# One transfer of 1 MB in place of two of 512 KB for the weight sums of each block unit

## The reference

```
def sq_relu_mlp(xn, w_in, w_out):
    h = jax.nn.relu(xn @ w_in)          # 1024 -> 4096
    return (h * h) @ w_out              # 4096 -> 1024

for i in range(2):
    h = h + attention_i(rms_norm(h, norm_mix_g[i]))
    h = h + sq_relu_mlp(rms_norm(h, norm_mlp_g[i]), mlp_w_in[i], mlp_w_out[i])
return rms_norm(h, norm_final_g)
```

## Time and profile before

| | before |
|---|---|
| median of 3 runs | 1864.57 us (1864.54 to 1865.13) |
| the profiled execution | 1863.85 us |
| its span, first to last instruction | 1862.1 us |
| PE busy | 1850.7 us, 99% of the span |
| DVE busy | 1311.2 us, 70% |
| ACT busy | 953.2 us, 51% |
| POOL busy | 222.8 us, 12% |
| granted clock of TensorE, mean | 0.999 |
| weight sums loaded by SP | 68 transfers of 512 KB, median 5.4 us from issue to landing |

### The profile page before, as it was taken

One profiled execution on the slowest core, in us unless ns is written; L12 is line 12 of the kernel. 1 busy time (PEld: TensorE's weight loads), 2 busy tenths in 40 slices (PEclk: granted clock), 3 DMA queues, 4 the chain that ended last, 5 costly groups with the idle time before them and its releaser, 6 DMA issues.

```text
span 1862.1 us, 28582 instructions
## 1 busy us (share of the span) xinstructions
PE 1850.7 (99%) x10747; PEld 1548.4 (83%) x10747; DVE 1311.2 (70%) x1816; ACT 953.2 (51%) x1222; POOL 222.8 (12%) x254
## 2 busy tenths in 40 slices
PE   9999999999999999999999999999999999999998
PEld 7788878888888887877888999988778788999997
DVE  7767775677357757556575788887788658588878
ACT  6392464545234343544443555555667754456464
POOL 0011122212211123111200000002101220000000
PEclk9999999999999999999999999999999999999999
DMA  6226213897888538786454353538335642435441
GB/s 243 90 83 194 68 65 94 208 216 176 201 204 204 125 110 200 164 192 159 138 134 158 112 194 119 187 114 221 110 102 153 141 132 96 153 119 187 144 179 69
DMA packets 128085, 277.43 MB, mean 149 GB/s; under 512 B 7389, under 2 KB 78941, under 8 KB 121696
## 3 DMA queue, kind: packets, MB, share of 16 engines
q1 hardware_dynamic: 95744, 187.19, 29.5%
q0 software_dynamic: 31936, 88.41, 22.7%
q10 hardware_dynamic: 288, 0.26, 0.0%
HBM read 271.53 MB, written 73.51 MB: 185 GB/s over the span
## 4 chain that ended last, share of the span: by engine, by line
PE 95%; DVE 2%; ACT 1%; DMA 1%; issue 0%; ACTq 0%; DVEq 0%
PE bank L1191 21%; PE bank L1189 21%; PE bank L1190 21%; PE bank L1629 6%; PE bank L1630 6%; PE bank L1631 6%; PE bank L1317 2%; PE bank L1934 2%; PE bank L1916 1%; DMA raw<-in_a_w_qkv 1%; PE bank L1323 1%; PE bank L1805 1%; PE bank L1806 1%; PE bank L1807 1%; PE bank L1793 1%; PE bank L1740 1%
## 5 line engine op out<-in xcount | busy, mean ns | idle before, releaser
L1189 PE MATMUL bank<-n_hi,w_hi 128*128 128x512 f32 x1054 | 425.0, 403 | 1.3 <-DVE w_lo L2030 1.3
L1191 PE MATMUL bank<-n_hi,w_lo 128*128 128x512 f32 x1054 | 417.9, 396 | 0.0
L1190 PE MATMUL bank<-n_lo,w_hi 128*128 128x512 f32 x1054 | 416.9, 396 | 0.0
L2024 ACT ACTIVATE w_hi<-raw 128x2048 fp32r<-128x2048 f32 (+2 forms) x111 | 207.4, 1868 | 343.0 <-PE bank L1191 327.5
L2030 DVE TENSOR_TENSOR w_lo<-raw,w_hi 128x2048 fp32r<-128x2048 f32 (+2 forms) x117 | 261.6, 2236 | 107.9 <-ACT w_hi L2024 106.0
L1190 PE MATMUL bank<-ff_lo,w_hi 128*128 128x512 f32 x688 | 271.6, 395 | 0.0
L1191 PE MATMUL bank<-ff_hi,w_lo 128*128 128x512 f32 x624 | 248.8, 399 | 0.0
L1189 PE MATMUL bank<-ff_hi,w_hi 128*128 128x512 f32 x624 | 245.2, 393 | 0.0
L1189 PEld LDWEIGHTS bank<-n_hi,w_hi 128*128 128x128 f32 x1054 | 198.0, 188 | 54.1 <-issue 5.0
L1190 PEld LDWEIGHTS bank<-n_lo,w_hi 128*128 128x128 f32 x1054 | 198.1, 188 | 48.8 <-issue 2.9
L1191 PEld LDWEIGHTS bank<-n_hi,w_lo 128*128 128x128 f32 x1054 | 197.9, 188 | 46.7
(11 more groups left out here) (467 smaller groups left out, 3319.1 us busy)
## 6 DMA issues: line engine op xcount, KB each, us to landing
weight_sums<-in_mlp_in POOLq DMA_DIRECT2D x72, 512.0 KB, 8.7
consts<-weight_sums SPq DMA_DIRECT2D x68, 512.0 KB, 5.4
raw<-in_w_up SPq DMA_DIRECT2D x22, 1024.0 KB, 7.3
raw<-in_mlp_out SPq DMA_DIRECT2D x22, 1024.0 KB, 4.8
raw<-in_mlp_in SPq DMA_DIRECT2D x24, 768.0 KB, 5.7
weight_sums<-weight_sums POOLq DMA_DIRECT2D x68, 256.0 KB, 5.9
weight_sums<-in_mlp_out POOLq DMA_DIRECT2D x30, 512.0 KB, 9.0
raw<-in_w_units SPq DMA_DIRECT2D x14, 1024.0 KB, 4.8
```

Source lines behind the costliest of these rows:

```text
L1189: nc.tensor.matmul(b[:, :], w_hi[:, j % 2, cols], hi, start=start, stop=False)
L1190: nc.tensor.matmul(b[:, :], w_hi[:, j % 2, cols], lo, start=False, stop=False)
L1191: return nc.tensor.matmul(b[:, :], w_lo[:, j % 2, cols], hi, start=False, stop=final)
L2024: act.activation(w_hi[:, s, cols], raw[:, s, cols], ACT.Copy).then_inc(hi_ready, 1)
```

## The change

Each block unit's sums come by one transfer of 1 MB, issued when both halves of the home are free, with one semaphore for each home in place of one for each home and half. ACT waits for the whole transfer ahead of either half.

```
-        sums_loaded, sums_made = {(i, op): sem("%s_loaded%d" % (op, i)) for i in range(2) for op in ("S23", "S14")}, sem("sums_made")
+        sums_loaded, sums_made = [sem("sums_loaded%d" % i) for i in range(2)], sem("sums_made")
...
         def summed(eng, m, op, u):
             i = sums_place(u)
-            eng.wait_ge(sums_loaded[i, op], 16 * sum(sums_place(v) == i and n <= SUM_ROW[m, u] for (_, v), n in SUM_ROW.items()))
+            eng.wait_ge(sums_loaded[i], 16 * sum(sums_place(v) == i and n <= SUM_ROW[m, u] for (_, v), n in SUM_ROW.items()))
...
                 for op in ("S23", "S14"):
                     sums_home_free(sp, m, op, u)
-                    to, cols = sum_piece(op, u), slice(0, 2 * SEQ) if op == "S23" else slice(2 * SEQ, 4 * SEQ)
-                    sp.dma_start(to, t["weight_sums"][SUM_ROW[m, u], :, cols]).then_inc(sums_loaded[sums_place(u), op], 16)
+                sp.dma_start(s_parts[sums_place(u)], t["weight_sums"][SUM_ROW[m, u]]).then_inc(sums_loaded[sums_place(u)], 16)
```

## The result

The changed kernel takes 1873.4 us in the median of six runs (1871.57 to 1874.29), the kernel before 1864.66 (1864.01 to 1865.4): a ratio of 1.0045, 95% interval 1.0034 to 1.0057, or 8.4 us (6.3 to 10.6). Losses in us are here the ratio times the kernel before; the two medians differ by 8.7. The forecast was 12.2 us slower, by a stall of TensorE at four places. The stalls are there, at those places, and are shorter than forecast. The profiled execution took 1874.29 us (span 1872.4), 10.4 us above the profiled one of before. One line went out of the code, so lines behind it are one lower (L2193 was L2194).

The account below looks back on a forecast made before the run. TensorE, busy 99% of the span, was taken to bound the kernel. Four border stalls of 2.5, 2.6, 4.2 and 2.9 us, together 12.2, on a median of 1864.6 gave 1876.8 us, range 1873 to 1881 (chance 0.62).

Parts of the forecast that it names:

- No idle time to win: Around the border of m = 1 and 2, TensorE is busy for all 34.00 us, so no gain can come there.
- SP's issue free: Removing 34 issues on SP, some 0.3 us each, 11 us in all, counts as nothing: SP is off the chain.
- 26 units covered: Units other than the four LATE and unit 0 after each: the longer transfer is covered and costs nothing.
- LATE: At four LATE units the transfer starts later; at the first border DVE moves 0.5 us, S1 in time by 0.4 us.
- Unit 0: Unit 0 of m = 2, 3, 6, 7: the late transfer delays S23, then A22 queued behind it; TensorE stalls 2.5 us at first.
- L1 + L2 - 7.8: TensorE's stall before A22 of unit 0 at each border: 2.5, 2.6, 4.2 and 2.9 us, together 12.2 us.
- L1: Time for 1 MB to land at the four LATE units: 4.9, 5.1, 5.6, 5.2 us.
- L2: Time for 1 MB to land at unit 0 after each LATE unit: 5.4, 5.3, 6.4, 5.5 us.
- the hidden rival: At the borders the longer transfer is hidden, perhaps helped by 8 KB rows: no change, 1864.6 us; chance 0.05.
- Half the stall: Rival: transfers take 4.7 us at each place, no cost of followers; 6.4 us slower, 1871.0 us; chance 0.13.
- Shared queue: Rival: at both transfers the second half adds 2.5 us, not 1.0; 12 us more, 1889 us; chance 0.08.
- The clock's fall: Rival: each of the four stalls brings the lower clock level; 9 us more, 1886 us; chance 0.10.

Follow-up runs that it names:

- the run with those units whole: Kernel before, with one 1 MB transfer for 26 units, two of 512 KB for the four LATE units and unit 0 after each: 1864.27 us, ratio 1.0002.
- the run with LATE alone: Kernel before, with one 1 MB transfer only for the four LATE units, the rest loaded as before: 1864.23 us, ratio 1.0002.
- the run of two transfers: Kernel before, two 512 KB transfers with a semaphore each, but both issued only when both halves are free: 1867.31 us, ratio 1.0017.
- the run with two rows of 4 KB: Changed kernel, the 1 MB described as two rows of 4 KB per partition; packets stayed as in the changed kernel: 1874.67 us, ratio 1.0054.
- The run with 5.4 us: Changed kernel, SP issuing unit 0's 1 MB after a LATE unit only when TensorE has ended LATE's last product: 1894.02 us, ratio 1.0159.

## Why the prediction was right, and where its size was off

*No idle time to win, SP's issue free, 26 units covered.* Right: the run with those units whole is at 1.0002.

*LATE.* Right in its mechanism: at the first border the low part of `S14` ended 6.62 us after LATE's first matmul in place of 6.17, so DVE moved by 0.45 us (forecast 0.5), S1 of LATE was in time, and the run with LATE alone loses nothing. The first matmul before and after, and the low part of `S14` after (1083.72 before):
```profile
1078.78 0.28 PE L1629 MATMUL bank<-ff_hi,w_hi 128*128 128x256 f32 x1
```
```profile
1078.49 0.28 PE L1628 MATMUL bank<-ff_hi,w_hi 128*128 128x256 f32 x1
```
```profile
1083.89 1.22 DVE L2193 TENSOR_TENSOR w_lo<-consts,w_hi 128x1024 fp32r<-128x1024 f32 x1
```

*Unit 0.* Right: place, releaser and order of the queues. The stall as L1 + L2 - 7.8 holds with the landings put in: at the first border 4.80 + 4.85 - 7.8 = 1.85, measured 1.94, and at the others it is as near, 0.1 us short. That nothing is late behind it holds as well. ACT's waits for sums are the 8 forecast: seven in the row below and the 7.36 us put down to TensorE, 43.3 us in all (forecast some 44).
```profile
ACT w_hi L2187 <- DMA consts<-weight_sums: 35.9, 7, 7.5
```
One sign failed: the granted clock did not stay at 1.00.

*The terms L1 and L2 are what was mis-sized.* I added 1.0 us for the second 512 KB to what a second half took in one execution, follower included: 4.9 to 5.6 and 5.3 to 6.4. They measured 4.7 to 4.9 and 4.8 to 5.1. So 1 MB beside followers lands nearly like the 1 MB of plain weights, and the 5.4 us of the third unit 0 were that execution's (4.1 to 4.7 us in three other runs with two halves there). The runs show a reason that I named under the hidden rival and put into no sum: the two halves went in packets of 4 KB, the whole goes in packets of 8 (SP's queue moves the same 187 MB in 90848 packets, before in 95744). With 4 KB the 1 MB takes 5.3 to 5.9 us, within my figures; that run also has the halves 2 KB apart, and which of the two counts isn't parted. With the measured landings the sum is 38.9 - 4 x 7.8 = 7.7 us, 1872.3.

*The rivals.* Half the stall (4.7 us each) lies nearer than the forecast, 6.4 against 12.2 to a measured 8.4, and what sets it apart, no cost of followers, is what the landings show. Place, wait and order are the same in both. Shared queue and no change are out (for the shared queue the 2.5 us are more than twice the 1.0 us that they are argued from; with 2.0 it would be 1885, as far off). The clock's fall was no rival to the stall but a term on top: once in four in this profile, at 1.5 us in place of the 2.3 I had worked out from the kernel's start, and not in all four. It is luck that such a fall, which the sum leaves out, makes up for part of the stall that the sum has too much. Whether the six runs, 2.7 us apart, differ by it isn't shown, as only one has a trace. Their mean granted clocks point that way: the three at 1.000 took 1871.57 to 1872.96 us, near the 1872.3, the three at 0.998 or 0.999 took 1873.84 to 1874.29.

The Trainium skill's rule to coalesce ("DMA: Bandwidth & Descriptors", "Rules for kernel authors") holds for the landing: 1 MB in one went faster than its two halves back to back (4.8 against 5.0 us from the first issue, at the first LATE unit of the run of two transfers; at the other seven places 4.7 to 5.1 against 5.0 to 7.3, at one of them no faster). The same table's advice to issue early and to wait late is what the change gave up.

What stays open: why in three profiles with stalls of 1.4 to 2.4 us the clock fell behind the third stall and behind no other. The length of the stall alone doesn't decide it: in the run with two rows of 4 KB it fell behind a third stall of 2.0 us and not behind a fourth of 2.4. The first matmul after these two stalls, and the windows behind them:
```profile
1692.19 0.38 PE L1629 MATMUL bank<-ff_hi,w_hi 128*128 128x256 f32 x1 [1.85 <-DVE w_lo L2194]
...
1779.05 0.39 PE L1629 MATMUL bank<-ff_hi,w_hi 128*128 128x256 f32 x1 [2.21 <-DVE w_lo L2194]
```
```profile
1693.40:1696.40 3.00, 3.00 (x16) 0.50 0.63 250
1779.10:1782.10 3.00, 3.00 (x25) 1.00 0.74 268
```

## What to carry to other kernels

Joining two transfers also joins their start conditions and their waits: ask for each half when its place comes free and when it is needed, and cost the join only where these lie close, not by bytes. Then follow the engines' written order behind the late piece, since what waits can be a neighbour whose own data are long there, as `A22` was; moving two splits, on DVE one of them past four additions, gave all of the 8.4 us back here. A stall of 2 us and more of TensorE can also cost a stretch at half clock behind it, 1.3 to 2.5 us here.

## What was not expected of the hardware

The prediction had a fall of the clock as a rival only. The granted clock went to 0.50 behind a standstill of only 2.0 us (idle time in the row 1.83), once in four; behind 2.8 to 3.0 us three times in four, behind 5.4 us four times in four. After a fall matmuls of 256 columns start 0.21 us apart in place of 0.12. The Trainium skill's page "TensorE: Matmul & The Clock Gate", section "HAM oscillation", tells of a kernel whose clock falls at every wait for a transfer, waits of 3 to 5 us there. The run with 5.4 us agrees; the shorter stalls here, of 2.0 to 3.0 us, show falls too, but only behind some.

A 1 MB load from device memory in packets of 4 KB, from rows in two parts 2 KB apart, landed 0.6 and 0.7 us later than in packets of 8 KB at the first border (5.4 and 5.6 against 4.8 and 4.9), and 0.5 later in the median of the eight places.
